# Forgetting-attention softmax rows scaled by the reciprocal of their sum on ScalarE, four operations, in place of one of VectorE

## The reference

```
logits = einsum('bqhd,bkhd->bhqk', q_block, k) * 64**-0.5 + F_q - F_k     # F: running sum of log forget gates
logits = where(causal mask, logits, -inf)
w      = softmax(logits, axis=-1)
out    = einsum('bhqk,bkhd->bqhd', w, v)
```

## Time and profile before

| | |
|---|---|
| median of 3 runs | 1081.15 us |
| the profiled execution, its own time | 1081.66 us |
| span of that execution (first to last instruction) | 1079.9 us |
| granted TensorE clock over the span | 0.997 of full speed |
| busy: PE / DVE / ACT / POOL | 98% / 69% / 54% / 7% |

### The profile page before, as it was taken

How to read it: one execution, slowest core, us unless ns; L and a number is a source line. 1 busy time by engine, 2 the same in 40 slices (tenths; PEclk the granted TensorE clock), 3 DMA queues, 4 the chain that set the end, 5 groups by cost and what they waited for, 6 DMA issues and landing times.

```text
span 1079.9 us, 22276 instructions
## 1 busy us (share of the span) xinstructions
PE 1062.4 (98%) x8792; PEld 1031.0 (95%) x8792; DVE 749.0 (69%) x1103; ACT 580.8 (54%) x881; POOL 75.7 (7%) x89
## 2 busy tenths in 40 slices
PE   7999999999999999999999999999999999999998
PEld 6899898999999999999999999898899999999998
DVE  6889898657776665667666667658767876666566
ACT  3555755476565554556544454454656665454454
POOL 0001000000420000021000001050000310000010
PEclk8999999999999999999999999999999999999999
DMA  5445433334556554565555456464334555554563
GB/s 213 144 167 176 157 116 135 146 103 172 185 190 210 194 194 158 185 203 189 204 191 194 152 184 223 183 196 157 117 118 157 182 177 207 189 191 171 188 223 118
DMA packets 32301, 187.81 MB, mean 174 GB/s; under 512 B 3817, under 2 KB 7537, under 8 KB 14449
## 3 DMA queue, kind: packets, MB, share of 16 engines
q1 hardware_dynamic: 31328, 185.58, 49.4%
q0 software_dynamic: 416, 1.06, 0.4%
q10 hardware_dynamic: 496, 0.33, 0.1%
HBM read 184.98 MB, written 1.06 MB: 172 GB/s over the span
## 4 chain that ended last, share of the span: by engine, by line
PE 85%; DVE 11%; ACT 3%; issue 1%; DMA 0%; DVEq 0%; ACTq 0%
PE acc L635 79%; DVE wlo L1515 4%; PE area_t L635 3%; PE area_a L635 3%; ACT whi L1126 1%; ACT s_a L1126 1%; DVE s_sum L2073 1%; DMA posi<-in_pos 0%; DVE st L1703 0%; ACT f_p L1126 0%; PE area_t L899 0%; DVE score L1745 0%; DVE f_sc L1965 0%; DVE work L1758 0%; DVE st L1756 0%
## 5 line engine op out<-in xcount | busy, mean ns | idle before, releaser
L635 PE MATMUL acc<-hs,whi 128*128 128x256 f32 x3584 | 624.1, 279 | 4.8 <-DVE wlo L1515 3.6
L635 PEld LDWEIGHTS acc<-hs,whi 128*128 128x128 f32 x3584 | 541.6, 187 | 11.6 <-issue 5.2
L635 PE MATMUL acc<-hs,wlo 128*128 128x256 f32 x1792 | 497.0, 277 | 0.0
L1126 ACT ACTIVATE whi<-raw 128x1024 fp32r<-128x1024 f32 (+3 forms) x379 | 356.7, 977 | 160.7 <-PE acc L635 134.5
L1515 DVE TENSOR_TENSOR wlo<-raw,whi 128x1024 fp32r<-128x1024 f32 (+4 forms) x259 | 273.0, 1096 | 104.3 <-ACT whi L1126 103.2
L635 PEld LDWEIGHTS acc<-hs,wlo 128*128 128x128 f32 x1792 | 336.1, 188 | 0.2
L635 PE MATMUL acc<-hid,whi 128*128 128x256 f32 x1056 | 181.0, 277 | 0.2 <-DVE wlo L1515 0.2
L635 PEld LDWEIGHTS acc<-hid,whi 128*128 128x128 f32 x1056 | 159.4, 188 | 0.4 <-DVE wlo L1515 0.4
L635 PE MATMUL acc<-hid,wlo 128*128 128x256 f32 x528 | 146.1, 277 | 0.0
L1604 DVE TENSOR_TENSOR wlo<-raw,whi 128x1024 fp32r<-128x1024 f32 x120 | 141.2, 1218 | 4.3 <-ACT whi L1126 4.2
L1617 DVE TENSOR_TENSOR hbuf<-acc,sbuf 128x256 f32<-128x256 f32 x66 | 28.0, 425 | 115.4 <-PE acc L635 112.1
(11 more groups left out here) (318 smaller groups left out, 1061.1 us busy)
## 6 DMA issues: line engine op xcount, KB each, us to landing
raw<-in_w_gu SPq DMA_DIRECT2D x66, 1024.0 KB, 4.7
raw<-in_w_dn SPq DMA_DIRECT2D x48, 704.0 KB, 4.0
raw<-in_w_up SPq DMA_DIRECT2D x10, 1024.0 KB, 4.8
raw<-in_w_gates1b SPq DMA_DIRECT2D x8, 1024.0 KB, 4.7
raw<-in_w_out SPq DMA_DIRECT2D x8, 1024.0 KB, 4.8
raw<-in_w_qk SPq DMA_DIRECT2D x8, 1024.0 KB, 4.9
raw<-in_w_gates SPq DMA_DIRECT2D x8, 1024.0 KB, 4.8
raw<-in_w_projT_b SPq DMA_DIRECT2D x7, 1024.0 KB, 4.8
```

The lines of the kernel that those rows point to most:

```text
L635: return nc.tensor.matmul(out, w, m, start=start, stop=stop, skip_group_check=True)
L1126: return nc.scalar.activation(out, in_, f, **kw)
```

## The change

In the `fox_p` steps VectorE issues the reciprocal alone, which now counts up a semaphore of its own (`fox_rec`), and does not wait for its result. ScalarE, which had nothing to do in these steps, waits for that semaphore and issues four activations of the form copy with a per-row scale, one a head, the last of which counts up `fox_probs`. The arithmetic is the same. The first attention steps of the first block (`dsa_p`, `mla_p`) stay as they were.

```diff
@@ ScalarE, step(name)
                     exps("fox", f_sc, f_p, tt, 2 * hg + tt + 1)
+                elif name.startswith("fox_p"):
+                    act.wait_ge(S("fox_rec"), softmaxes_before(name) + 1)
+                    ks = keys(int(name[-1]))
+                    for h in range(4):
+                        m = fn(f_p[:, h, 0:ks], f_p[:, h, 0:ks], ACT.Copy, scale=softmax_columns("fox")[2][:, h:h + 1])
+                    m.then_inc(S("fox_probs"), 1)
                 elif name.startswith("sb_s"):
@@ VectorE, step(name)
                     dve.wait_ge(S(f"{tag}_exp"), softmaxes_before(name) + 1)
+                    if tag == "fox":
+                        v.reciprocal(rec, sums).then_inc(S("fox_rec"), 1)
+                        return
                     link(v.reciprocal(rec, sums))
                     ks = keys(int(name[-1]))
-                    p = {"dsa": d_p, "mla": m_p, "fox": f_p}[tag][:, :, 0:ks]
+                    p = {"dsa": d_p, "mla": m_p}[tag][:, :, 0:ks]
```

## The result

| | median of 6 runs | lowest to highest |
|---|---|---|
| before | 1081.05 us | 1080.04 to 1081.21 |
| after | 1089.38 us | 1088.42 to 1090.42 |

The ratio is 1.0079, 95% interval 1.0068 to 1.0089. The forecast of 1087.9 us had the direction, and the time lies in its range (1085.3 to 1091.8), but inside the range it lies between the forecast and rival 1. The profiled execution took 1089.55 us with a span of 1087.7 us.

A forecast was written before the change was run, and what follows sets the result against it. TensorE, busy 98% of the span, was taken as the bound. Delays of 5.4 us at the scores of `sb_s10` and 1.3 us at `fox_p11` made 6.7 us: 1081.15 + 6.7 = 1087.9 us, range 1085.3 to 1091.8.

The forecast's parts named there:

- rival 1: TensorE's clock falls to half speed in the new pause before `sb_t01`: 3.0 us more, 1090.9 us; chance 0.33.
- The size of an activation: ScalarE's activations on `f_p` start 0.30 us apart for 128x128 and 0.40 us for 128x256.
- Step a: At `fox_p00`: four activations ahead of the splits of G0 make them 1.2 us later.
- Step b: At `fox_p01`: four activations ahead of `s_pt` add 1.6 us; VectorE's splits of G2 go 2.8 us later.
- Step c: At `fox_p10`: ScalarE waits for a reciprocal behind `sb_m01`; `sb_x01` 5.95 us late, TensorE pauses 3.9 us, scores 5.4 us late.
- Step d: At `fox_p11`: transposes of `fox_t11` go 1.7 us later, 0.42 us wait for G7 is swallowed: +1.3 us.
- The sum: Over the whole stretch: 5.4 us at the scores of `sb_s10` plus 1.3 us at `fox_p11`, 6.7 us.
- Rivals 2 and 3: 2: ScalarE has room, 1080.6 us, chance 0.06. 3: delays before `fox_p10` overlap instead of adding, 1085.1 us, chance 0.10.

The follow-up runs named there:

- s_ab: The changed kernel with only `fox_p00` and `fox_p01` scaled by ScalarE, the other two by VectorE as before: 1083.69 us, +2.8 us over before.
- p10_const: The changed kernel with `fox_p10` scaled by a column of ones, without the wait for the reciprocal: 1083.93 us, +3.0 us over before.
- p10_late: The changed kernel with `fox_p10` later in the list, ahead of `sb_m10`: 1084.18 us, +2.9 us over before.
- s_d: The changed kernel with only `fox_p11` scaled by ScalarE: 1082.38 us, +1.5 us over before.
- warm: The changed kernel with 8 more `keep_warm` matmuls filling the pause ahead of the transposes of `sb_t01`: 1088.02 us, +6.8 us over before.
- again: The changed kernel run once more, nothing altered: 1089.47 us, +8.2 us over before.
- s_c: The changed kernel with only `fox_p10` scaled by ScalarE: 1085.61 us, +4.7 us over before.
- plain: The changed kernel with constant scale 1.0 in all sixteen activations in place of a per-row column, rows left undivided: 1088.65 us, +7.6 us over before.
- s_c_warm: s_c with 8 more `keep_warm` matmuls ahead of the transposes of `sb_t01`, filling the pause: 1084.45 us, +3.4 us over before.

## Why the prediction was right, and where it was short

- **The size of an activation.** 0.30 and 0.40 us were taken; 0.29 and 0.40 came (1.17 and 1.59 us for four). Right.
- **Step a**, +1.2 us: VectorE's splits of G0 came 747.43 - 747.24 + 0.97 = 1.16 us late. Right.
- **Step b**, +2.8 us: VectorE's splits of G2 came 767.32 - 765.55 + 0.97 = 2.74 us late, and s_ab costs +2.8 us. Right.
- **Step c**, +5.95 us at `sb_x01`: 779.58 - 774.65 + 0.97 = 5.9 us. The cause, that the reciprocal stands behind `sb_m01`, is shown by p10_const and p10_late. Of the pause of 3.9 us, 4.15 came. Up to the start of the transposes right; the 5.4 us at the scores became 7.9, since the clock had fallen.
- **Step d**, +1.3 us: the transposes of `fox_t11` wait 1.56 us, the 0.42 us before G7 are gone, and s_d costs +1.5 us. Right.
- **The sum**, 6.7 us: warm costs 6.8, and by its timeline the scores of `sb_s10` come 784.20 - 779.11 + 0.23 = 5.3 us late, against 5.4. Steps a, b and d alone (p10_const, p10_late) would be 2.8 + 1.3 = 4.1 less what the missing multiplication gives back, 0.53, so 3.6; measured 3.0 and 2.9, a little under, with 3.6 inside both intervals. By the timelines the scores of `sb_s10` come 2.2 us late in both kernels (780.32 and 780.64, with the exponential at 738.03 and 738.38), against 2.8 - 0.53 = 2.3, and the transposes of `fox_t11` wait 1.56 us as in the changed kernel.
- **Rival 1** was the mis-sized part. The forecast proper left it out at a chance of 0.33, but the clock fell in or just behind the pause in all four profiled executions that had it unfilled (after, again, s_c and plain), and in neither of the two that had it filled (warm, s_c_warm). Of the eleven runs of the changed kernel seven have a mean granted clock of 0.995 or less; warm, in five runs, has none under 0.997. Its price was set at 3.0 us: the profiled execution lost 2.6, the medians 1.4. So the likeliest case held the clock term at 0 where 1.4 was due. The price had also taken one length of the slow stretch, 6.9 us: in s_c and plain it was 3.4 us, which would explain a median under 2.6, but the unprofiled runs do not show its length.
- **The range.** Its upper part was there for rival 1, and what put the time above the forecast was rival 1. That 1089.38 us lies also just inside the forecast's own range (1086.3 to 1089.5) is luck: that range stood for the size of the activations, which came as taken, and what filled it was the clock.
- **Rivals 2 and 3** fall. There was no room where it counted, and the delays of steps a and b did reach the reciprocal.
- Behind this stretch the view of waits lists none of TensorE in either profile, and from its first matmuls on G7 to its last row it takes 262.2 us before and 261.9 now. So next to nothing was given back, as forecast.
- **Two slips in the working.** By the earlier trace rows the clock was back at 15.46 and not at 15.54 (0.77 in that microsecond is 0.46 at half speed), so the first slow stretch is 6.8 and not 6.9 us. And four groups at 0.4 us less each are 1.6 and not 1.5 us, so the lower bound is 5.1 us. Neither changes the forecast.

What stays open: the four runs with a mean clock of 0.997 or 0.998 (1088.42 to 1089.20 us) lie 0.9 us over warm's median too. A single slow stretch explains such a mean, be it at the start or in the pause, and the mean does not tell which.

## What to carry to other kernels

Before work is moved to an engine that is "only 54% busy", look at what stands behind it in that engine's queue, and at where the semaphore that it will wait for is counted up in the other engine's queue. Here 3.8 us of work left VectorE from places where three of four were hidden anyway, and a result of 0.17 us, issued 3 us too late, held up everything on ScalarE, then TensorE, then TensorE's clock. The same step 12 us later costs 5 us less, with the same work.

## What was not expected of the hardware

- The slow stretch after a pause began at different times and had different lengths: from 779.2 to 786.0 in the changed kernel and from 779.7 to 786.5 in again, but from 780.0 to 783.4 in s_c and from 780.1 to 783.5 in plain, after pauses of 4.15, 3.94, 3.94 and 3.57 us. In s_c it began 1.3 us after work had started again.
- The same kernel's start has such a stretch in some executions and not in others: of the 18 runs of before beside warm, 6 had a mean clock of 1.0. The profiled execution of p10_late had a granted clock of 1.0 over the span, the one of before 0.997.
- Two executions come apart by over 1 us before the change is even reached: in the twelve profiles the same exponential of `fox_s00` starts between 738.03 and 739.43. The place of the slow stretch at the start does not explain it, as shown above.
